# Output weights' third unit, the opening's sum of squares and the order of weighing in the attention core rearranged

## The chip, the cores and the metric

The kernel runs on one core of one Trainium2 chip. The metric is the device time of one execution in microseconds (us), the median of several runs. A matrix engine (PE), a vector engine (DVE), a scalar engine (ACT), a general engine (POOL) and a queue that starts transfers (SP) work side by side, each through its own instructions in order, and wait for each other by semaphores.

## What is computed

An encoder trunk of two layers on 272 tokens (256 and 16 learned meta tokens) of width 1024. Layer 0 is FFN, attention (16 query heads, 4 key/value heads of 64, rotary positions), FFN; layer 1 is FFN, a recurrent block, FFN. Cut to what matters here:

```python
h = concatenate([meta, x])                       # 272 x 1024
for layer in range(2):
    h = h + 0.5 * rms_norm(swiglu(rms_norm(h, g[0]), ffn_w_in, ffn_w_out), g[1])
    hn = rms_norm(h, g[2])                       # layer 0: attention
    q, k, v = split(hn @ w_qkv)
    q, k = rope(rms_norm(q, q_gain)) / 8, rope(rms_norm(k, k_gain))
    o = softmax(q @ k.T) @ v                     # 16 heads
    h = h + rms_norm(o @ w_o, g[3])
    h = h + 0.5 * rms_norm(swiglu(rms_norm(h, g[4]), ffn_w_in, ffn_w_out), g[5])
```

All arrays are float32. `rms_norm` needs the mean of the squares of h over the 1024 channels of each token.

## The kernel before

Activations lie with channels on the 128 partitions: `h[:, c, :]`, c = 0 to 7, holds 272 tokens. A product in full precision is made of three matmuls of split operands (`product`, L473 to L475): a high part (xh, wh) and a low part (xl, wl). Weights come in units of up to 1 MB through a ring of four slots: SP loads `raw`, ACT copies it to `wh` (`high`, L981), DVE subtracts to get `wl` (`low`, L1394), and PE multiplies. A slot is loaded again when the `low` of its last unit is done. U_QKV+0 to +5 are the six units of the q, k and v weights, U_WO+0 to +3 the four of the output weights.

**Opening.** ACT splits h and the first four units and squares the eight tiles of h (`h_square`, L993) into a buffer of two; POOL adds the squares one after the other into `hacc` (`sum_squares`, L1887 and L1890). PE takes the mean over the partitions (`mean_of_h`, L527) behind the gate half of the third tile of the first FFN and goes on with the up half, inside which it spreads the reciprocal root over the partitions (`spread_r`, L520). The scaled tiles (L1463, L1464) that free PE's banks need that spread.

**Queries and keys.** Tiles t = 0 to 9 (two of keys, eight of queries) are multiplied in order; inside the product of a later tile PE takes the head means (`head_means`, L727) and the rotation (`rotate`, L737) of an earlier one. DVE follows per tile with `head_root_in`, `times_sin`, `head_factor`, ACT with `squared` and `root`, POOL with `times_cos` and `roped`. Copies and subtractions of later weight units are set between these by hand: `low(U_QKV + 4, 0)` after t = 3, `high(U_WO, ...)` before `root(4)`.

**Attention core.** 18 steps. Steps 0 and 9 treat the 16 last query rows of eight heads; the other 16 are pairs of steps, two token halves of one tile of two heads. Step s on PE: `scores(s + 2)` (L764, or L756 for steps 0 and 9), `turn(s)` (six transposes of the softmax rows, three in steps 0 and 9, L775), `weigh(s - 1)` (values times probabilities, 12 records, L787). Step s on DVE: `normalise(s)` (L1657, L1661), for every second step `out_split` (L1665, L1667), then `maximum(s + 2)` (L1644) and `shifted(s + 2)` (L1652). Step s on ACT: `exponents(s + 1)` (L1215), then `place(s)` (L1234; L1227 and L1228 for steps 0 and 9). `scores(s)` waits for `exponents(s - 2)`, the second half of `turn(s)` for `place(s - 1)`, `weigh(s)` for `place(s)`, and `place(9)` for all of the first eight weighings. In the last two steps PE begins the output projection between turns (`begin_wo`). The third output unit is copied by ACT in step 0 and subtracted by DVE in step 10, where DVE also clears `acc` (L1421).

Of the kernel before, what the change touches and what calls it, by code (L numbers as in the profile page):

```python
# [9 lines left out]
ALU = mybir.AluOpType  # L10
# [7 lines left out]
KC = D // P  # L18
# [54 lines left out]
STEPS_S = 9  # L73
# [81 lines left out]
def build(nc, x, meta, gains, ffn_in, ffn_out, w_qkv, q_gain, k_gain, w_o, rec_in, conv_w, conv_b,  # L155
          gate_w, gate_b, lam, rec_out, consts, out):
    ctx = ExitStack()
    with ctx:
# [309 lines left out]
        def _(pe):  # L468
# [230 lines left out]
            def attention():  # L699
# [150 lines left out]
                for s in range(STEPS):  # L850
                    if s + 2 < STEPS:
                        scores(s + 2)
                    if s == 0:
                        pe.wait_ge(q_step, 3 * QKT - 2)
                        pe.wait_ge(q_sin, QKT)
                        pe.wait_ge(v_ready, 2)
                    if s >= STEPS - 2:
                        begin_wo(3 * (s - STEPS + 2), 3 * (s - STEPS + 2) + 3)
                    turn(s)
                    if s == 0:  # L860
                        pe.wait_ge(v_ready, 4)
                    if s >= 1 and (s - 1) % STEPS_S:
                        weigh(s - 1)
                begin_wo(6, 7)
                weigh(STEPS - 1)

            def begin_wo(k0, k1):
# [107 lines left out]
        def _(act):  # L975
# [12 lines left out]

            def h_square(n, c):
                t0 = PROJ_T0[n - 1] if n else 0  # L990
                if 8 * n + c >= 2:
                    act.wait_ge(hacc_step, 8 * n + c - 1)
                act.activation(sqh[:, c % 2, t0:L], h[:, c, t0:L], ACT.Square).then_inc(hsq_ready, 1)  # L993

            def make_x(n):

# [160 lines left out]
            def attention():  # L1157
                def squared(t):

                    act.wait_ge(qk_done, t + 1)  # L1160
                    if t >= 2:
                        act.wait_ge(q_sum, t - 1 if t % 2 or t == 2 else t)
                    for a, cols in row_parts(t) if t >= KT_N else ((t % 2 * L, slice(0, L)),):
                        last = act.activation(qs_row[:, a:a + cols.stop - cols.start], qk_bank(t)[:, cols], ACT.Square)
                    last.then_inc(q_squared, 1)
                    if t >= 2:
                        act.wait_ge(q_rot, t - 1)
                        act.wait_ge(q_cos, t - 1)
                    g = 1 if t < KT_N else 0
                    act.activation(qp[:, t % 2, :], qk_bank(t)[:, 0:L], ACT.Copy, scale=qg[:, g:g + 1]).then_inc(q_gained, 1)  # L1170

                def root(t):
                    act.wait_ge(q_step, 3 * t + 1)
                    if t < KT_N:
                        v = hs[:, t].rearrange("p c g -> p (c g)")
                    else:
                        a, n = factor_columns(t)
                        v = hq[:, a:a + n]
                    act.activation(v, v, ACT.Sqrt, bias=EPS).then_inc(q_root, 1)

                squared(0)
                squared(1)
                root_of_h(1)
                high(U_QKV + 4, 0, KC, (qk_done, 4))
                act.wait_ge(norm_q_sum, 1)
                act.activation(rc_q[:, :], SUM_PRE[:, SC + 3:SC + 8], ACT.Sqrt, bias=EPS).then_inc(norm_q_root, 1)
                root(0)
                squared(2)
                root(1)
                squared(3)  # L1190
                high(U_QKV + 5, 0, KC, (qk_done, 4))
                root(2)
                squared(4)
                root(3)
                squared(5)
                high(U_WO, 0, KC, (qk_done, 6))
                root(4)
                squared(6)
                root(5)
                root(6)  # L1200
                squared(7)
                high(U_WO + 1, 0, KC, (qk_done, 8))
                root(7)
                squared(8)
                root(8)
                squared(9)
                root(9)
                load_table(ACT.Exp)

                def exponents(s):  # L1210
                    act.wait_ge(shift_ready, s + 1)
                    if s >= 2:
                        act.wait_ge(t_done, first_tile(s - 1))
                    for e, a in enumerate(range(first_tile(s), first_tile(s + 1))):
                        act.activation(prow[:, 2 * (s % 2) + e, :], SCORE[s % 2][:, e, 0:L], ACT.Exp,  # L1215
                                       scale=hq[:, factor_column(a):factor_column(a) + 1], bias=shift[:, a:a + 1],
                                       accum_out=rsum[:, a:a + 1]).then_inc(p_exp, 1)

                def place(s):

                    p, q = divmod(s, STEPS_S)
                    act.wait_ge(t_done, first_tile(s + 1))
                    if q == 0:
                        if p:
                            act.wait_ge(pv_done, 4 * p)
                        src = flipped[0:KT, TURN[s][0][1], 0:3 * P].rearrange("p (c j g q) -> p c j g q", c=3, j=2, g=GROUP)
                        act.activation(pt[:, 0, :, :, 2 * P:L], src[:, :, 0], ACT.Copy)  # L1227
                        act.activation(pt[:, 1, :, :, 2 * P:L], src[:, :, 1], ACT.Copy).then_inc(pt_ready, 1)  # L1228
                    else:
                        j, i, half = pair_of(s)  # L1230
                        b0, b1 = sorted(b for e, b, placed in TURN[s])
                        src = flipped[0:KT, b0:b1 + 1, 0:3 * P].rearrange("p g (c q) -> p g c q", c=3)
                        dst = pt[:, j % 2, :, i:GROUP:2, P * half:P * half + P].rearrange("p c g q -> p g c q")
                        act.activation(dst, src, ACT.Copy).then_inc(pt_ready, 1)  # L1234

                exponents(0)
                for s in range(STEPS):
                    if s + 1 < STEPS:
                        exponents(s + 1)
                    if s == 0:  # L1240
                        high(U_WO + 2, 0, KC, (qk_done, 10))
                    place(s)
                high(U_WO + 3, 0)
                load_table(ACT.Sqrt)
# [113 lines left out]
                x_high(0, c)  # L1358
            high_half(1, 0)
            high_half(1, 1)  # L1360
            h_square(0, 0)
            h_square(0, 1)
            high(2, 0)
            high(3, 0)
            for c in range(2, KC):
                h_square(0, c)
            ffn(0, True)

# [20 lines left out]
        def _(dve):  # L1389
# [13 lines left out]
            def rc_of_h(n):  # L1403
                dve.wait_ge(pre_root, n + 1)
                dve.reciprocal(rc_pre[:, :], rc_pre[:, :]).then_inc(rc_ready, 1)
# [166 lines left out]
            def attention():  # L1572
# [30 lines left out]
                def final(t):  # L1603
# [5 lines left out]
                dve.wait_ge(hacc_step, 8 * 1 + 8)  # L1609
                dve.tensor_copy(hrest[:, :].rearrange("p (i m) -> p i m", i=2),  # L1610
                                hacc[:, L - META:L].rearrange("p (o m) -> p o m", o=1).broadcast_to([P, 2, META])).then_inc(rest_doubled, 1)
                rc_of_h(1)
                dve.wait_ge(rc_ready, 2)
                dve.tensor_tensor(rsq[:, :], rc_pre[:, :], rc_pre[:, :], ALU.mult).then_inc(rsq_ready, 1)
# [7 lines left out]
                for t in range(QKT - 1):  # L1622
                    head_root_in(t)
                    times_sin(t)
                    head_factor(t)
                    if t == 1:
                        final(0)
                    if t == 2:
                        final(1)
                    if t == 3:  # L1630
                        low(U_QKV + 4, 0)
                    if t == 5:
                        low(U_QKV + 5, 0)
                    if t in (6, 7):
                        low(U_WO + t - 6, 0)
# [37 lines left out]
                head_factor(QKT - 1)  # L1673
                maximum(1)
                shifted(1)
                value(0)
                value(1)
                for s in range(STEPS):
                    normalise(s)
                    if s == 0:  # L1680
                        value(2)
                        dve.wait_ge(v_ready, 3)
                        dve.memset(vt[0:OVERLAP, 2, :], 0.0).then_inc(v_ready, 1)
                    if s == 10:
                        low(U_WO + 2, 0)
                        clear_sum()
                    if s >= 2 and (s - 2) % STEPS_S:
                        j, i, half = pair_of(s - 2)
                        if half:
# [142 lines left out]
            def low_half(u, i):  # L1832
# [3 lines left out]
                last = dve.tensor_tensor(wl[:, slot(u), cols], raw[:, slot(u), cols], wh[:, slot(u), cols].bitcast(F32), ALU.subtract)  # L1836
                last.then_inc(w_ready if i else w_half, 1)

            def copy_h(c):
                dve.wait_ge(x_trans, c + 1)  # L1840
                dve.tensor_copy(h[:, c, :], bank[4 + c % 4][:, 0:L]).then_inc(h_ready, 1)
# [15 lines left out]
            dve.tensor_scalar(vec_h[:, :], vec_a[:, :], 0.5, None, ALU.mult).then_inc(vec_ready, 1)  # L1857
            low(2, 0)
            low(3, 0)

            ffn(0, True)
            attention()
# [13 lines left out]
        def _(pool):  # L1876
            def sum_squares(n):

                t0 = PROJ_T0[n - 1] if n else 0
                if n:  # L1880
                    pool.wait_ge(pre_sum, n)
                if n == 2:
                    pool.wait_ge(norm_q_sum, 1)
                for c in range(KC):
# [59 lines left out]
                y_sum(2)  # L1944
                y_gated(2)

            sum_squares(0)
            sum_squares(1)
            rotary()
            sum_squares(2)  # L1950
# [30 lines left out]
```

## Time and profile before

| | |
|---|---|
| median of 3 runs | 1075.98 us (1074.69 to 1076.16) |
| the profiled execution | 1076.33 us, its span 1074.5 us |
| PE busy | 1055.3 us, 98% of the span |
| DVE, ACT, POOL busy | 683.3, 545.4, 91.3 us |
| moved by transfers | 170.15 MB, mean 158 GB/s |
| mean granted clock of PE | 0.996 of full |

The span is from the first to the last instruction of the profiled execution. Times in the rows are microseconds from its start. A busy PE is not one at its peak: the modelled end of a matmul lies behind the start of the next, so durations of PE blocks are best taken from start to start.

### The profile page before, as it was taken

How to read it: one execution, taken by the hardware profiler on the slowest of the kernel's cores; microseconds unless marked ns; L12 is line 12 of the kernel's file. 1: busy time of each engine (PE TensorE's matmuls, PEld its weight loads, DVE VectorE, ACT ScalarE, POOL GpSimd, SP SyncE). 2: the span in 40 equal slices, each digit the busy share in tenths (PEclk: the TensorE clock that was granted, in tenths of full speed). 3: DMA queues.
4: the chain of work that ended last, by engine and by line, in shares of the span. 5: the costliest groups of instructions: out<-in, count | busy, mean ns of one | idle time of the engine just before them, and what ended most of it. 6: DMA issues, size and time to landing. Idle time of an engine off the chain costs nothing.

```text
span 1074.5 us, 20606 instructions
## 1 busy us (share of the span) xinstructions
PE 1055.3 (98%) x8416; PEld 1026.4 (96%) x8416; DVE 683.3 (64%) x991; ACT 545.4 (51%) x790; POOL 91.3 (8%) x92
## 2 busy tenths in 40 slices
PE   9999999999989999999999999999999999999997
PEld 8899999999879999999999999999999999999986
DVE  6566656467664866664457666644698668667652
ACT  5544444454765544444346444444569845454541
POOL 2100000028000200000011000000223310000000
PEclk9999999999989999999999999999999999999999
DMA  9465446625013255435563555366328525655541
GB/s 301 154 225 165 137 138 209 218 89 175 27 41 123 95 188 185 156 122 188 193 204 118 173 193 164 108 203 217 118 80 269 162 80 182 200 167 197 189 143 39
DMA packets 160910, 170.15 MB, mean 158 GB/s; under 512 B 3264, under 2 KB 154104, under 8 KB 160840
## 3 DMA queue, kind: packets, MB, share of 16 engines
q1 hardware_dynamic: 160456, 168.70, 48.0%
q8 instruction: 51, 0.84, 0.3%
q0 software_dynamic: 96, 0.28, 0.1%
q10 hardware_dynamic: 288, 0.18, 0.1%
q14 instruction: 19, 0.16, 0.0%
HBM read 167.82 MB, written 1.05 MB: 157 GB/s over the span
## 4 chain that ended last, share of the span: by engine, by line
PE 89%; DVE 4%; ACT 2%; DMA 2%; SPq 1%; POOL 1%; issue 1%; DVEq 0%; POOLq 0%; ACTq 0%
PE bank L473 23%; PE bank L475 23%; PE bank L474 23%; PE bank L882 5%; PE bank L681 2%; PE bank L680 2%; PE bank L682 2%; PE weighed L787 1%; PE bank L492 1%; PE bank L489 1%; PE flipped L775 1%; PE bank L490 1%; DMA raw<-in_ffn_w_in 1%; DVE h L1436 1%; DMA raw<-in_rec_w_in 1%; POOL hacc L1890 1%
## 5 line engine op out<-in xcount | busy, mean ns | idle before, releaser
L1394 DVE TENSOR_TENSOR wl<-raw,wh 128x2048 fp32r<-128x2048 f32 (+2 forms) x164 | 340.5, 2097 | 152.7 <-ACT wh L981 152.2
L473 PE MATMUL bank<-xh,wl 128*128 128x272 f32 (+1 forms) x1488 | 431.1, 290 | 3.4 <-DVE tmp L1464 1.1
L475 PE MATMUL bank<-xh,wh 128*128 128x272 f32 (+1 forms) x1488 | 428.0, 288 | 0.0
L474 PE MATMUL bank<-xl,wh 128*128 128x272 f32 (+1 forms) x1488 | 426.3, 286 | 0.0
L981 ACT ACTIVATE wh<-raw 128x2048 fp32r<-128x2048 f32 (+2 forms) x164 | 282.2, 1745 | 104.6 <-PE bank L475 82.9
L473 PEld LDWEIGHTS bank<-xh,wl 128*128 128x128 f32 x1488 | 280.9, 189 | 5.2 <-issue 2.7
L474 PEld LDWEIGHTS bank<-xl,wh 128*128 128x128 f32 x1488 | 281.0, 189 | 0.0
L475 PEld LDWEIGHTS bank<-xh,wh 128*128 128x128 f32 x1488 | 280.7, 189 | 0.0
L473 PE MATMUL bank<-ah,wl 128*128 128x272 f32 x528 | 152.5, 289 | 0.0
L474 PE MATMUL bank<-al,wh 128*128 128x272 f32 x528 | 152.2, 288 | 0.0
L475 PE MATMUL bank<-ah,wh 128*128 128x272 f32 x528 | 151.8, 287 | 0.0
L1047 ACT ACTIVATE tmp<-tmp 128x272 f32<-128x272 f32 (+1 forms) x88 | 37.7, 428 | 215.3 <-DVE tmp L1463 215.0
L474 PEld LDWEIGHTS bank<-al,wh 128*128 128x128 f32 x528 | 99.5, 188 | 0.0
L473 PEld LDWEIGHTS bank<-ah,wl 128*128 128x128 f32 x528 | 99.5, 188 | 0.0
L475 PEld LDWEIGHTS bank<-ah,wh 128*128 128x128 f32 x528 | 99.4, 188 | 0.0
L1482 DVE TENSOR_TENSOR al<-tmp,ah 128x272 f32 (+3 forms) x88 | 38.2, 438 | 51.0 <-ACT ah L1052 50.4
L1463 DVE TENSOR_TENSOR tmp<-bank,r 128x272 f32<-128x272 f32 (+1 forms) x88 | 38.1, 433 | 50.4 <-PE bank L475 50.3
L1887 POOL COPY hacc<-sqh 128x272 f32<-128x272 f32 (+1 forms) x6 | 2.9, 488 | 700.4 <-ACT sqh L993 700.4
L1052 ACT ACTIVATE ah<-tmp 128x272 f32 (+3 forms) x88 | 37.4, 428 | 47.4 <-DVE tmp L1472 47.4
L489 PE MATMUL bank<-xh,wl 128*128 128x272 f32 (+1 forms) x176 | 46.1, 290 | 2.3 <-ACT xh L987 1.7
L1472 DVE TENSOR_TENSOR tmp<-tmp 128x272 f32<-128x272 f32 (+1 forms) x88 | 38.2, 437 | 13.6 <-ACT tmp L1047 9.2
L490 PE MATMUL bank<-xh,wh 128*128 128x272 f32 (+1 forms) x176 | 45.6, 287 | 0.0
(199 smaller groups left out, 1207.7 us busy)
## 6 DMA issues: line engine op xcount, KB each, us to landing
raw<-in_ffn_w_in SPq DMA_DIRECT2D x88, 1024.0 KB, 5.3
raw<-in_ffn_w_out SPq DMA_DIRECT2D x24, 768.0 KB, 4.4
raw<-in_ffn_w_out SPq DMA_DIRECT2D x24, 640.0 KB, 3.8
raw<-in_ffn_w_out SPq DMA_DIRECT2D x10, 1024.0 KB, 5.2
raw<-in_rec_w_in SPq DMA_DIRECT2D x8, 1024.0 KB, 5.5
raw<-in_attn_w_qkv SPq DMA_DIRECT2D x6, 1024.0 KB, 5.0
raw<-in_attn_w_o SPq DMA_DIRECT2D x4, 1024.0 KB, 5.0
raw<-in_rec_gate_w SPq DMA_DIRECT2D x16, 256.0 KB, 5.0
```

Source lines behind the costliest of these rows:

```text
L473: pe.matmul(dst, b, mh, start=first, stop=False)
L474: pe.matmul(dst, a, ml, start=False, stop=False)
L475: return pe.matmul(dst, a, mh, start=False, stop=last)
L489: pe.matmul(dst, b, xh[:, k, t0:L], start=k == 0, stop=False)
L490: pe.matmul(dst, a, xh[:, k, t0:L], start=False, stop=False)
L882: done = pe.matmul(dst[:, cols], w, x[:, cols], start=first and half == 0, stop=last, skip_group_check=True)
L981: act.activation(wh[:, slot(u), 0:kn * 256], raw[:, slot(u), 0:kn * 256], ACT.Copy).then_inc(wh_ready, units)
L1047: act.activation(sl[:, b, t0:L], gp[:, b, t0:L], ACT.Silu).then_inc(silu_done, 1)
L1394: dve.tensor_tensor(wl[:, slot(u), 0:kn * 256], w, wh[:, slot(u), 0:kn * 256].bitcast(F32), ALU.subtract).then_inc(w_ready, units)
L1463: dve.tensor_tensor(gp[:, b, t0:L], bank[banks[0]][:, t0:L], r[:, t0:L], ALU.mult).then_inc(gate_scaled, 1)
L1472: dve.tensor_tensor(aa[:, b, t0:L], sl[:, b, t0:L], up[:, b, t0:L], ALU.mult).then_inc(a_full, 1)
L1482: dve.tensor_tensor(d, aa[:, b, t0:L], s, ALU.subtract).then_inc(a_ready, 1)
```

## The change

In the opening, the squares of h go to eight places of `tmp` without waiting for one another, all of them behind the copies of units 2 and 3; DVE adds them in three instructions (`first_sum`) behind its subtractions of units 2 and 3, and POOL no longer takes part. In the q and k stage, `root(4)` stands ahead of `high(U_WO)` on ACT and `low(U_QKV + 4)` moves behind tile 4 on DVE. `clear_sum` moves to the beginning of the attention stage. The third output unit's copy moves ahead of `root(9)` on ACT, its subtraction ahead of `value(0)` on DVE. In the core, PE weighs the two halves of a tile one right behind the other: nothing in the first step of a pair's weighing, two in the second.

```diff
-                    if s >= 1 and (s - 1) % STEPS_S:
+                    q = (s - 1) % STEPS_S
+                    if s >= 1 and q and q % 2 == 0:
+                        weigh(s - 2)
                         weigh(s - 1)
                 begin_wo(6, 7)
+                weigh(STEPS - 2)
                 weigh(STEPS - 1)
...
             def h_square(n, c):
                 t0 = PROJ_T0[n - 1] if n else 0
-                if 8 * n + c >= 2:
-                    act.wait_ge(hacc_step, 8 * n + c - 1)
-                act.activation(sqh[:, c % 2, t0:L], h[:, c, t0:L], ACT.Square).then_inc(hsq_ready, 1)
+                if n:
+                    act.wait_ge(hacc_step, 8 * n + max(c - 1, 0))
+                dst = sqh[:, c % 2, t0:L] if n else tmp[:, c, :]
+                act.activation(dst, h[:, c, t0:L], ACT.Square).then_inc(hsq_ready, 1)
...
                 squared(5)
+                root(4)
                 high(U_WO, 0, KC, (qk_done, 6))
-                root(4)
...
                 squared(9)
+                high(U_WO + 2, 0, KC, (qk_done, 10))
                 root(9)
...
-                    if s == 0:
-                        high(U_WO + 2, 0, KC, (qk_done, 10))
                     place(s)
...
-            h_square(0, 0)
-            h_square(0, 1)
             high(2, 0)
             high(3, 0)
-            for c in range(2, KC):
+            for c in range(KC):
                 h_square(0, c)
...
+                clear_sum()
                 rc_of_h(1)
...
-                    if t == 3:
+                    if t == 4:
                         low(U_QKV + 4, 0)
...
                 shifted(1)
+                low(U_WO + 2, 0)
                 value(0)
...
-                    if s == 10:
-                        low(U_WO + 2, 0)
-                        clear_sum()
...
+            def first_sum():
+
+                dve.wait_ge(hsq_ready, KC)
+                dve.tensor_tensor(tmp[:, 0:4, :], tmp[:, 0:4, :], tmp[:, 4:8, :], ALU.add).then_inc(hacc_step, 1)
+                dve.wait_ge(hacc_step, 1)
+                dve.tensor_tensor(tmp[:, 0:2, :], tmp[:, 0:2, :], tmp[:, 2:4, :], ALU.add).then_inc(hacc_step, 1)
+                dve.wait_ge(hacc_step, 2)
+                dve.tensor_tensor(hacc[:, :], tmp[:, 0, :], tmp[:, 1, :], ALU.add).then_inc(hacc_step, KC - 2)
...
             low(2, 0)
             low(3, 0)
+            first_sum()
...
-            sum_squares(0)
             sum_squares(1)
```

## Rows read from the trace of the kernel before

**Rows 1.** The page, part 4: share of the last chain by engine.
```profile
PE 89%; DVE 4%; ACT 2%; DMA 2%; SPq 1%; POOL 1%; issue 1%; DVEq 0%; POOLq 0%; ACTq 0%
```

**Rows 2.** PE's waits, whole span: total us, times, longest us.
```profile
PE flipped L775 <- DVE prow L1661: 2.9, 2, 2.5
...
PE bank L473 <- DVE tmp L1464: 1.1, 1, 1.1
...
PE score_odd L764 <- ACT prow L1215: 0.4, 1, 0.4
```

**Rows 3.** Timeline of the opening: start, us, instruction, count, idle before and releaser.
```profile
19.97 1.92 ACT L981 ACTIVATE wh<-raw 128x2048 fp32r<-128x2048 f32 x1 [0.47 <-DMA raw<-in_ffn_w_in]
21.79 0.73 ACT L993 ACTIVATE sqh<-h 128x272 f32<-128x272 f32 x2
...
21.87 4.48 DVE L1394 TENSOR_TENSOR wl<-raw,wh 128x2048 fp32r<-128x2048 f32 x2
...
22.28 9.26 POOL L1890 TENSOR_TENSOR hacc<-hacc,sqh 128x272 f32<-128x272 f32 x6 [3.43 <-ACT sqh L993]
...
29.87 0.29 PE L475 MATMUL bank<-xh,wh 128*128 128x272 f32 x1
31.60 0.67 PE L527 MATMUL bank<-cst,hacc 128*96 128x1 f32 x6 [1.44 <-POOL hacc L1890]
```

**Rows 4.** Timeline of the q and k stage, DVE and PE.
```profile
251.13 2.28 DVE L1394 TENSOR_TENSOR wl<-raw,wh 128x2048 fp32r<-128x2048 f32 x1
...
252.89 0.29 PE L475 MATMUL bank<-xh,wh 128*128 128x272 f32 x1
253.63 0.58 PE L727 MATMUL bank<-cst,tmp 128*128 128x2 f32 x4 [0.45 <-DVE hq L1581]
```

**Rows 5.** Timeline of DVE and PE around step 10, and where the projection begins.
```profile
300.22 2.28 DVE L1394 TENSOR_TENSOR wl<-raw,wh 128x2048 fp32r<-128x2048 f32 x1
...
305.01 1.49 PE L775 MATMUL flipped<-cst,prow 128*96 128x128 f32 x6 [2.52 <-DVE prow L1661]
...
318.47 0.40 PE L473 MATMUL bank<-xh,wl 128*128 128x272 f32 x1
```

**Rows 6.** Stretches: length; PE, PEld, DVE, ACT, POOL busy; clock; transfers' share; GB/s.
```profile
282.00:298.00 16.00, 15.86 (x184) 12.04 (x182) 13.63 (x43) 13.40 (x35) 0.00 (x0) 1.00 0.01 2
...
304.00:308.00 4.00, 2.99 (x20) 2.28 (x20) 2.57 (x10) 2.69 (x8) 0.00 (x0) 0.51 0.73 251
```

**Rows 7.** Timeline of DVE and ACT where the moved work comes to stand.
```profile
237.16 0.17 DVE L1405 RECIPROCAL rc_pre<-rc_pre 96x3 f32<-96x3 f32 x1 [2.14 <-ACT rc_pre L1003]
...
273.68 0.16 DVE L1652 TENSOR_TENSOR shift<-nmax,hq 128x2 f32<-128x2 f32 x1
275.91 0.87 DVE L1639 TENSOR_SCALAR vt<-bank,rc_pre 96x256 f32<-96x256 f32 x2 [2.08 <-PE bank L803]
...
270.73 0.21 ACT L1179 ACTIVATE hq<-hq 128x5 f32<-128x5 f32 x1 [1.62 <-DVE hq L1581]
```

**Rows 8.** Timeline of PE in the core: undisturbed steps, then step 9.
```profile
286.47 0.73 PE L764 MATMUL score_even<-kd,qt 64*128 64x136 f32 x8
287.13 0.86 PE L775 MATMUL flipped<-cst,prow 128*96 128x128 f32 x6
287.92 0.88 PE L787 MATMUL weighed<-pt,vt 96*64 96x128 f32 x12
288.73 0.73 PE L764 MATMUL score_odd<-kd,qt 64*128 64x136 f32 x8
...
298.52 0.53 PE L775 MATMUL flipped<-cst,prow 128*96 128x128 f32 x3
298.99 0.96 PE L787 MATMUL weighed<-pt,vt 96*64 96x144 f32 x12
```

**Rows 9.** Groups by shape, 282 to 298 us: count, busy us, mean ns, idle before.
```profile
L1234 ACT ACTIVATE pt<-flipped 96x768 f32<-96x768 f32 x8 | 6.4, 806 | 2.8 <-PE flipped L775 2.8
L1215 ACT ACTIVATE prow<-score_even,shift,hq 128x272 f32<-128x272 f32 x7 | 3.9, 569 | 0.0
```

More of the change, by code:

```diff
@@ L1877, in sum_squares @@
             def sum_squares(n):
-                t0 = PROJ_T0[n - 1] if n else 0
-                if n:
-                    pool.wait_ge(pre_sum, n)
+                t0 = PROJ_T0[n - 1]
+                pool.wait_ge(pre_sum, n)
                 if n == 2:
```

## The prediction

> **What bounds the kernel now.** I read the chain of waits first: 89% of the chain that ended last is PE [rows 1]. So an edit pays only where it shortens PE's own work or one of its stalls, and the next view is PE's list of waits [rows 2]: the longest is for the normalised softmax rows, 2.9 us in two waits, 2.5 in one. Then I read the timeline at each stall that the change touches.
>
> In the opening, PE's mean of the squares starts at 31.60 after 1.44 idle, released by POOL, whose six last additions take 9.26 us from 22.28 [rows 3]. In the q and k stage PE is held 0.45 for DVE's root input, which stood behind the subtraction of a unit (251.13, 2.28 us) [rows 4]. In the core the 2.52 before the turn of step 11 ends at 305.01, and DVE's step 10 began with a subtraction of 2.28 us at 300.22 [rows 5]. After that idle stretch the granted clock in 304 to 308 is 0.51, near the 1.2 GHz level, so the stall is paid again in slow matmuls [rows 6].
>
> **Opening.** Without the wait the mean would start one matmul spacing behind 29.87; spacing there is 0.13 us (0.29 is the modelled duration, with overlap), so at 30.00, against 31.60: 1.60 us. Will the sum be ready? ACT's copy of unit 3 waits for its transfer and runs 19.97 to 21.79 (start of the next); eight squares at the spacing of 0.31 that two of them show (0.73 in all, 0.43 for one) take 2.6, to 24.4. DVE is busy with units 2 and 3 until 26.35, so DVE decides. Its three additions have 1088, 544 and 272 elements a partition. The trace has 2048 in 2.24 each (4.48 for two) and small ones of 272 at about 0.44; on a line between them these are 1.26, 0.72 and 0.44, with dependency gaps 2.5 us in all: `hacc` at 28.9, 1.1 before PE wants it. The copies of units 2 and 3 and their subtractions don't get later, because two squares leave ACT ahead of them. Everything behind the mean hangs on PE's own place in its program (the spread stands at the sixth product of the up half), so the 1.1 wait for the scaled tile [rows 2] stays and only moves. Bounds: 1.44 (the idle time only) to 1.60; I take 1.60.
>
> **Queries and keys.** The mean at 253.63 would follow 252.89 by 0.13: 0.61 us to gain. With unit QKV+4 moved behind tile 4, `head_root_in(4)` runs at once at 251.2, `times_sin(4)` to 251.8, `root(4)` no longer behind a 1.9 us copy; all before PE arrives at 253.02. The subtraction then runs from about 252.1 to 254.4. Its weights are wanted by tile 8, behind the mean, rotation and the 27 matmuls left of tiles 6 and 7 (3.4), so not before 257.5. The next root input waits for the subtraction, to 254.4, while PE asks for it 12 matmuls (1.5) into tile 7, near 256. What POOL does meanwhile may be held up by the two-input subtraction as it was before, with over a microsecond to spare. Bounds 0.45 to 0.61; I take 0.60.
>
> **Clearing and the third output unit.** The clear (0.28 us) falls into DVE's 2.14 idle before 237.16 [rows 7]: nothing. On ACT the copy (1.9) stands ahead of the last root, which began at 270.73 [rows 7]: the copy takes the place of the 1.62 idle before it, and the root comes about 0.2 later than it could. Its user is the normalisation of the first softmax row, which stands behind two values that wait for PE: hidden. On DVE the subtraction starts after the shift of step 1 (273.68 [rows 7], now 0.6 earlier) and needs 2.28 to 275.4, and DVE's next instruction there waited 2.08 for PE anyway: nothing. If that cover failed, up to the length of the subtraction, 2.2, less PE's slack before its first turn, would come back.
>
> **The stall in the core.** Blocks from start to start: scores 0.66, turn 0.79, weighing of a first half 0.81 [rows 8], of a second half 0.89 (16 more columns in 12 records). The weighing at 298.99 ends 0.89 later, at 299.87. From there to the projection at 318.47 [rows 5] PE has six scores and turns, 6 x 1.45 = 8.70, and five weighings, 3 x 0.81 + 2 x 0.89 = 4.21: 12.91 us. One wait of about 0.4 for the exponents of step 11 [rows 2] isn't DVE's doing and stays. 299.87 + 12.91 + 0.42 = 313.20, so stall and slow clock together cost 318.47 - 313.20 = 5.27 us. All of it goes if nothing takes its place; bounds 4.9 to 5.7 (the second if the 0.4 goes too).
>
> **Weighing in one run.** A turn of three transposes takes 0.47 (298.52 to 298.99), one of six 0.79 [rows 8]: 0.107 a transpose, and 0.15 once per block. The weighings likewise: 0.08 for 12 x 16 columns makes 5 ns for 12 columns, 12 x 128 columns are 0.64, so 0.17 per block is not columns; scores, 8 x 136, 0.45 of 0.66, leave 0.21. The six-transpose turn has a satisfied wait in its middle and pays nothing for it, so I put the 0.15 to 0.21 down to the change of shape between blocks, not to the waits. Two weighings, one right behind the other, drop one such change per tile: 8 x 0.17 = 1.36 us. Ends: 0 (if it belongs to the wait, which is kept) and 8 x 0.21 = 1.7.
> The Trainium skill, page "TensorEngine Tiling (Array Packing)", section Key Properties, says that changing the tiling mode, not the tile alone, drains the engine. By that rule the sum is as above; if the 0.17 belonged to the waits it would be 1.36 us higher. The rows agree with the rule as far as they go.
>
> Against it: PE has no weighing in the first step of a pair, and runs ahead of ACT and DVE. An ACT step is two exponents and their accumulator reads, 2 x 0.55 from start to start, and a placing of 0.81 (0.70 to the next) [rows 9], 1.8 us; two steps 3.6, against PE's 4.5 per tile: enough in the steady state. There turn to turn in the short step is 1.45, and the second half of the turn, 1.85 behind the last one's start, needs a placing that ends 0.90 + 0.81 = 1.71 behind it: 0.14 to spare. But at each of the two starts (steps 1 to 3 and 10 to 12) no earlier weighing covers the exponents, and PE now has one step more of 1.45 against ACT's 1.8 before its first weighing: it must wait 0.35 more, with the semaphore's way some 0.39, at the scores of step 3 and of step 12. Loss 2 x 0.39 = 0.78 us, bounds 0.2 (slack that I don't see) to 1.6 (each start pays twice).
>
> **Sum.** 1.60 + 0.60 + 5.27 + 1.36 - 0.78 = 8.05 us. The profiled execution's 1076.33 becomes 1068.3; it lies 0.35 above the median of 1075.98, so the median becomes 1068.0 rounded. Later stages are PE's and should only move: the transfer of the FFN's third unit starts earlier, since the slot is freed near 275.4 instead of 302.5.
>
> **Rivals.**
> A. *The short steps starve.* If the 0.17 belongs to the wait (+1.36) and each of the six other tiles also stands about 0.39 (+2.3), the time is 1071.7. For it: ACT is busy 13.4 of 16 us [rows 6], and the margin above is 0.14. Against: PE's steady period is still longer than ACT's.
> B. *The opening's sum is late.* If the additions started behind a later unit 3 or ran slower than the line says, PE's wait returns from 1.1 us of delay on, and whole from 2.7, which gives 1069.6. DVE's chain has 1.1 of slack, but rests on a transfer.
> C. *The moved unit hits the start of the core.* If its copy comes so late that the subtraction delays the values and the first turn, of its 2.2 us some 1.7 return (an estimate: PE's last 24 value matmuls hide the rest): 1069.7. For it: ACT's queue there is full (copy, root, table, exponents). Against: DVE's 2.08 of waiting [rows 7].
> D. *Slower.* PE's many small idle pieces in the new order let its clock fall to 1.2 GHz in the core. The trace shows the fall after 2.52 idle [rows 5, 6], with 5.27 - 2.52 = 2.75 us paid besides the idle time. The core's PE work is some 16 x 2.3 = 37 us; from 8.05 us of it at half clock the gain is gone, from 10.2 us the kernel is slower by 0.2%, a third of the core (12 us) gives 1080. Against: waits of 0.4 and 1.1 [rows 2] left the clock at full, and none of mine is above 0.4.
> That the change doesn't do what it says: only if the step 11 turn waits for something behind the subtraction; ACT's exponents 11 are the 0.4 already counted.
>
> **How the numbers follow.** Forecast 0.66, A 0.15, B 0.08, C 0.07, D 0.04. A measurement of this kernel tells about 0.2% (2.2 us) from no change. Worst ends of the terms: 1.44 + 0.45 + 4.9 + 0 - 1.6 = 5.2, time 1070.8; best: 1.60 + 0.61 + 5.7 + 1.7 - 0.2 = 9.4, time 1066.6. B and C lie inside; A and D, 0.19, are left out. Faster: all but D, 0.95 with a little taken off for mixtures; same 0.02, slower 0.03.
>
> **What would show it.** PE's wait for POOL in the opening gone and its mean at 30.0; no wait for DVE near 253; no subtraction in step 10 and the granted clock at full through the core; projection from about 310 (8.05 us less what comes after); weighing runs of 24 records in 1.53 us start to start; waits of 0.4 for exponents at steps 3 and 12 only. Wrong: a 24-record run of 1.70, waits for placings in every second turn, a clock below 1.00 between 276 and 322, or a wait for DVE's values at the first turn.

## The result, and the profile after

The changed kernel takes 1068.05 us (median of 4 runs, 1067.55 to 1068.81) against 1075.95 for the kernel before in the same set: a ratio of 0.993, 95% interval 0.9912 to 0.9947. The forecast was 1068.0. The profiled execution took 1068.51 us, 7.82 less than the one before. So the total was met; the terms behind it were not all.

PE's waits in the changed kernel (total us, times, longest us), which answer to [rows 2]:

```profile
...
PE flipped L775 <- ACT pt L1239: 1.2, 4, 0.4
PE bank L473 <- DVE tmp L1465: 1.1, 1, 1.1
PE bank L473 <- DVE xl L1669: 1.1, 1, 1.1
...
PE score_odd L764 <- ACT prow L1220: 0.7, 2, 0.4
PE flipped L775 <- DVE prow L1663: 0.4, 1, 0.4
...
PE score_even L764 <- ACT prow L1220: 0.3, 1, 0.3
```

The three waits that the change aimed at are gone: POOL's sum, DVE's root input, the 2.5 us in step 11. New are four waits for a placing, 1.2 in all, and two for exponents (the kernel before had one of 0.4). The rows left out stand in both kernels. The wait of 0.6 for the second unit's low part (L489) is no longer listed either.

**Opening.** Timeline of the changed kernel, against [rows 3]:

```profile
15.40 3.38 DVE L1401 SCALAR_TENSOR_TENSOR xl<-h,vec_a,xh 128x272 fp32r<-128x272 f32 x8
...
21.09 4.48 DVE L1395 TENSOR_TENSOR wl<-raw,wh 128x2048 fp32r<-128x2048 f32 x2
25.49 1.28 DVE L1842 TENSOR_TENSOR tmp<-tmp 128x1088 f32<-128x1088 f32 x1
26.81 0.73 DVE L1844 TENSOR_TENSOR tmp<-tmp 128x544 f32<-128x544 f32 x1
27.64 0.44 DVE L1846 TENSOR_TENSOR hacc<-tmp 128x272 f32<-128x272 f32 x1
...
21.02 2.66 ACT L997 ACTIVATE tmp<-h 128x272 f32<-128x272 f32 x8
...
29.21 0.59 PE L527 MATMUL bank<-cst,hacc 128*96 128x1 f32 x6
```

The sum costs DVE what was worked out (1.28, 0.73, 0.44) and is there 1.1 before PE. But the mean starts at 29.21, not at 30.00. The larger part of the difference stands in two rows of the kernel before that the prediction had not looked at:

```profile
15.49 4.07 DVE L1400 SCALAR_TENSOR_TENSOR xl<-h,vec_a,xh 128x272 fp32r<-128x272 f32 x8
...
20.75 0.39 PE L489 MATMUL bank<-xh,wl 128*128 128x272 f32 x1 [0.62 <-DVE wl L1836]
```

The eight low parts of x took DVE 0.69 longer there, and PE stood 0.62 for the unit subtracted behind them.

This is one pair of traces. Five experiments below keep the opening of the kernel before (e5, e6, e8, e10, e12). From the first low part of x to the mean, e5 and e12 take 16.08 and 16.11, like the 16.11 of the kernel before; e6, e8 and e10 take 15.45, 15.43 and 15.45, and in them the mean waits for POOL only 0.74 to 0.78. In the three slower ones POOL's first addition of the last six lasts 4.5 to 4.7, behind both subtractions of DVE. In the other three the copy of unit 3 did not wait for its transfer, and that addition was over in 0.77, when the subtractions began. The new opening takes 13.81 to 13.83 in every trace that has it. So it is worth 1.6 to 2.3, depending on the run.

**Queries and keys**, against [rows 4]:

```profile
248.88 0.20 ACT L1183 ACTIVATE hq<-hq 128x4 f32<-128x4 f32 x1 [0.34 <-DVE hq L1582]
...
250.50 2.28 DVE L1395 TENSOR_TENSOR wl<-raw,wh 128x2048 fp32r<-128x2048 f32 x1
...
250.56 0.50 PE L727 MATMUL bank<-cst,tmp 128*128 128x2 f32 x4
```

The head mean at 253.63 now starts at 250.56, 3.07 earlier. Of this 2.46 had been gained ahead of it (the mean of the tile before moved from 250.61 to 248.15); the rest is 0.61, as forecast.

**Core.** PE in the steady part, against [rows 8]:

```profile
283.61 0.73 PE L764 MATMUL score_even<-kd,qt 64*128 64x136 f32 x8
284.27 0.86 PE L775 MATMUL flipped<-cst,prow 128*96 128x128 f32 x6
285.06 0.73 PE L764 MATMUL score_odd<-kd,qt 64*128 64x136 f32 x8
286.09 0.83 PE L775 MATMUL flipped<-cst,prow 128*96 128x128 f32 x6 [0.29 <-ACT pt L1239]
286.85 1.61 PE L787 MATMUL weighed<-pt,vt 96*64 96x128 f32 x24
288.39 0.73 PE L764 MATMUL score_even<-kd,qt 64*128 64x136 f32 x8
```

The run of two weighings takes 1.54 start to start against 0.81 + 0.89, 0.16 saved. But the scores of the short step last 1.03 to the next turn instead of 0.66, and the tile takes 4.78 instead of 4.60. The stretch that held the stall, against [rows 6]:

```profile
304.00:308.00 4.00, 3.71 (x44) 2.84 (x41) 3.34 (x10) 3.02 (x10) 0.00 (x0) 1.00 0.00 0
```

The clock is at its full level (2.4 GHz).

One measure serves for the core from here on: the stretch from PE's scores of step 2 to its first product behind the last output split. Its ends are 278.62 and 329.42 before, 275.47 and 321.61 after, so 50.80 and 46.14 us. The 7.82 of the two profiled executions are then 2.39 in the opening, 0.07 on the way to the q and k stage, 0.61 in it, 0.08 on the way to the core and 4.66 in the core (7.81).

### The profile page after: what moved, and what is told of

Same layout as the page of the kernel before. It is cut to its first block, busy times and chain, and to the rows that moved or that the text cites. A ratio compares the mean times of both kernels' runs of the same rounds, so it can differ in the third digit from the quotient of the medians.

```text
span 1066.7 us, 20595 instructions
## 1 busy us (share of the span) xinstructions
PE 1050.5 (98%) x8416; PEld 1024.2 (96%) x8416; DVE 685.0 (64%) x994; ACT 544.2 (51%) x790; POOL 81.2 (8%) x84
## 3 DMA queue, kind: packets, MB, share of 16 engines
HBM read 167.82 MB, written 1.05 MB: 158 GB/s over the span
## 4 chain that ended last, share of the span: by engine, by line
PE 90%; DVE 4%; ACT 3%; DMA 1%; issue 0%; SPq 0%; DVEq 0%; ACTq 0%
PE bank L473 23%; PE bank L475 23%; PE bank L474 23%; PE bank L885 4%; PE bank L681 2%; PE bank L680 2%; PE bank L682 2%; PE bank L492 1%; PE bank L489 1%; DMA raw<-in_rec_w_in 1%; PE bank L490 1%; PE weighed L787 1%; DVE xl L1401 1%; PE flipped L775 1%; DVE h L1437 1%; PE bank L520 1%
## 5 line engine op out<-in xcount | busy, mean ns | idle before, releaser
L489 PE MATMUL bank<-xh,wl 128*128 128x272 f32 (+1 forms) x176 | 45.9, 289 | 1.9 <-ACT xh L990 1.7
```

What stands on the lines that cost most here:

```text
L489: pe.matmul(dst, b, xh[:, k, t0:L], start=k == 0, stop=False)
```

## The experiments

Where a trace is quoted, the stretch is the one just defined. The changed kernel ran once more beside the last set (**e9_changed_again**):

> The changed kernel itself, beside the others of this set. 1068.0, its stretch from the scores of step 2 to the product behind the last output split 46.1 us as before.

1068.27 us (1067.52 to 1068.96, 5 runs); stretch 321.28 - 275.16 = 46.12.

**e5_unit_only**: the kernel before with the moved unit and clearing alone.

```diff
                 squared(9)
+                high(U_WO + 2, 0, KC, (qk_done, 10))
                 root(9)
...
-                    if s == 0:
-                        high(U_WO + 2, 0, KC, (qk_done, 10))
...
+                clear_sum()
                 rc_of_h(1)
...
                 shifted(1)
+                low(U_WO + 2, 0)
...
-                    if s == 10:
-                        low(U_WO + 2, 0)
-                        clear_sum()
```

> The kernel before with only the third output unit (its copy on ACT, its subtraction on DVE) and the clearing moved. Theory of the stall: 5.27 us less, 1070.7, no wait before the turn of step 11, clock at full through the core, the first output product 5.3 earlier than 318.5. Rival: another wait in steps 10 to 12 takes its place and only part of it goes, over 1072.

1070.28 us (1070.11 to 1071.82), ratio 0.9954 (0.9938 to 0.9971). The stretch is 324.81 - 279.14 = 45.67, so 5.13 less than before. The list of waits has none left at the turn of step 11. The rival falls.

Three of its runs took 1070.11 to 1070.29, with a mean clock of 1.000; the profiled one took 1071.82, with 0.998. Its trace shows the difference, and it lies in the opening:

```profile
30.61 0.67 PE L527 MATMUL bank<-cst,hacc 128*96 128x1 f32 x6 [1.41 <-POOL hacc L1888]
...
32.00:34.00 2.00, 2.00 (x12) 2.00 (x11) 0.00 (x0) 1.98 (x2) 0.00 (x0) 0.52 0.07 20
34.00:36.00 2.00, 2.00 (x14) 2.00 (x13) 0.00 (x0) 0.81 (x2) 0.00 (x0) 0.62 0.00 0
```

Behind the wait of 1.41 for POOL's sum the clock fell to the 1.2 GHz level for some 3 us. From the mean to the scores of step 2 this run takes 279.14 - 30.61 = 248.53, the kernel before 278.62 - 31.60 = 247.02: the fall cost 1.5. In the kernel before the same wait of 1.44 left the clock at full:

```profile
32.00:34.00 2.00, 2.00 (x19) 2.00 (x19) 0.17 (x1) 1.70 (x2) 0.00 (x0) 1.00 0.29 89
```

**e1_alternate**: the changed kernel with the old order of weighing.

```diff
-                    q = (s - 1) % STEPS_S
-                    if s >= 1 and q and q % 2 == 0:
-                        weigh(s - 2)
+                    if s >= 1 and (s - 1) % STEPS_S:
                         weigh(s - 1)
                 begin_wo(6, 7)
-                weigh(STEPS - 2)
                 weigh(STEPS - 1)
```

> The changed kernel with PE's old order of weighing, one half a step; all else of the change stays. Theory P (as predicted): the run of two saves 1.36 us of shape changes and costs 0.78 in two waits, so without it the time goes up 0.6, to 1068.6. Theory W (from the changed kernel's trace): the run of two saves 0.16 a tile, 1.3 in all, but PE then stands 0.29 to 0.36 in four short turns (steps 5, 7, 9, 14) and about 0.7 in two starts, 1.9 in all; without it the time falls 0.6, to 1067.4. In the trace, from the scores of step 2 to the first product behind the last output split: P 46.7, W 45.5, the changed kernel 46.1. W also wants the four waits for placings gone.

The stretch is 320.79 - 275.12 = 45.67, and the waits for placings are gone; 1067.69 us (1067.59 to 1068.55). Theory W holds in direction. So the run of two cost 0.47 in the core, where the prediction had counted on a gain of 0.58. In time alone this can't be told (1067.69 against 1068.05 and 1068.27); the traces tell it.

**e2_mixed**: as e1, but the last two tiles in runs of two.

```diff
-                    q = (s - 1) % STEPS_S
-                    if s >= 1 and q and q % 2 == 0:
+                    if 1 <= s < STEPS - 3 and (s - 1) % STEPS_S:
+                        weigh(s - 1)
+                    if s == STEPS - 2:
                         weigh(s - 2)
                         weigh(s - 1)
```

> As e1_alternate, but the last two tiles (steps 14 and 15, 16 and 17) are weighed in one run, where PE has output products between the turns to cover ACT and DVE. Theory W: the two runs save 2 x 0.16 and cost nothing, so 0.3 below e1_alternate, 1067.1, with the stretch at 45.2. Theory P: each run of two pays everywhere, so still above the changed kernel, about 1068.3.

The stretch is 320.40 - 275.44 = 44.96; 1067.48 us (1067.39 to 1068.20), which the time alone can't tell from e1. The direction is W's, but the stretch is 0.71 below e1's, more than twice the 0.3 expected. The rows of step 15 show why. e1_alternate:

```profile
308.25 0.86 PE L775 MATMUL flipped<-cst,prow 128*96 128x128 f32 x6
309.04 0.88 PE L787 MATMUL weighed<-pt,vt 96*64 96x128 f32 x12
309.85 0.39 PE L473 MATMUL bank<-xh,wl 128*128 128x272 f32 x1
```

e2_mixed:

```profile
308.57 0.86 PE L775 MATMUL flipped<-cst,prow 128*96 128x128 f32 x6
309.19 0.37 PE L473 MATMUL bank<-xh,wl 128*128 128x272 f32 x1
```

A turn ahead of a weighing lasts 0.79 to the next start, one ahead of a product 0.62, which is no more than six times 0.107. From transposes to products (both on the whole array, 128 rows) nothing is paid. So with no weighing between them two changes of shape fall away instead of one: 0.17 + 0.17 for each of the two tiles, 0.7 in all. Both kinds of block stand behind a wait for a semaphore that holds nothing up here, so the 0.15 to 0.21 per block belongs to the change of shape and not to the wait. The Trainium skill, page "TensorEngine Tiling (Array Packing)", section Key Properties, has it that changing the mode, not the tile, drains the engine; the runs agree.

**e7_no_low_part**: which engine ends the wait in the short step?

```diff
+                    if pair < 2 * NKV - 1:
+                        dve.tensor_copy(xh[:, pair, :], weighed[:, 0:L]).then_inc(o_ready, 1)
+                        return
                     dve.tensor_copy(xh[:, pair, :], weighed[:, 0:L]).then_inc(oh_ready, 1)
...
```

> Leaves out the low part of the attention output (the subtraction at the output split) for all but the last tile, 0.44 us of DVE in every second step; the rest is the changed kernel. It tells which engine ends PE's wait in the short turns of steps 5, 7, 9 and 14. If it is DVE's normalisation, which stands behind output split and maximum, the waits of 0.29 to 0.36 shrink or go. If it is ACT's placing of the step before, which begins only when the turn before ends, they stay whole.

1069.82 us in its one run, which can't be set against the others; the stretch is 321.43 - 275.94 = 45.49, 0.65 less than in the changed kernel. Its timeline around step 5 (PE, DVE, ACT):

```profile
285.53 0.73 PE L764 MATMUL score_odd<-kd,qt 64*128 64x136 f32 x8
286.40 0.83 PE L775 MATMUL flipped<-cst,prow 128*96 128x128 f32 x6
...
284.86 0.72 DVE L1646 TENSOR_REDUCE nmax<-score_even 128x2 f32<-128x544 f32 x1 [0.22 <-PE score_even L764]
...
285.89 0.63 DVE L1663 TENSOR_SCALAR prow<-prow,rinv 128x272 f32<-128x272 f32 x2
...
285.64 0.81 ACT L1239 ACTIVATE pt<-flipped 96x768 f32<-96x768 f32 x1 [0.99 <-PE flipped L775]
```

For comparison DVE and ACT in the changed kernel, whose turn starts at 286.09:

```profile
283.73 0.44 DVE L1667 CAST xh<-weighed 128x272 fp32r<-128x272 f32 x1 [0.48 <-PE weighed L787]
...
285.58 0.63 DVE L1663 TENSOR_SCALAR prow<-prow,rinv 128x272 f32<-128x272 f32 x2
...
285.17 0.81 ACT L1239 ACTIVATE pt<-flipped 96x768 f32<-96x768 f32 x1 [0.98 <-PE flipped L775]
```

In e7 the turn starts at 286.40 while the placing still runs (to 286.45): its first half doesn't need it. It needs the first normalised row, which ends near 286.25. In the changed kernel both ended together (placing 285.98, normalised row 285.94), and the profile names the later; with less DVE work the scores' 1.03 became 0.87, and the maximum now waited for PE's scores instead of for DVE. So DVE's chain behind the run of two decides: output split 0.83, then maximum, shift, reciprocal and normalisation. In the changed kernel the turn starts 286.09 - 283.61 = 2.48 behind the end of the run of two, where PE's own way would be 0.66 + 0.79 + 0.66 = 2.11: 0.37 too late. All four waits shrank by 0.16 or so in e7, which makes its 0.65. The 0.21 that is left of each is DVE's too: the maximum stands ahead of the normalisation that the turn needs, and waits for PE's scores. Whether the placing of ACT would hold the turn's second half once DVE is out of the way was not tested.

**e8_weigh_only**: the kernel before with the run of two alone (the same edit as in the change).

> The kernel before with the weighing in runs of two as its only edit. Theory P: 0.6 faster, 1075.4. Theory W: 0.6 slower, 1076.5, with the waits for placings at the same steps; the big stall before the turn of step 11 stays about 2.5 long, since DVE's unit is still in step 10, and the clock falls as before.

1073.84 us (1072.23 to 1077.70, 10 runs), ratio 0.9995 (0.9982 to 1.0008): neither P nor W can be told from it, since its runs differ by more than both. The four waits for placings are there, and the stall is 1.98 long. And a part of my expectation failed: in the profiled run the clock did not fall.

```profile
304.00:306.00 2.00, 1.50 (x14) 1.14 (x14) 1.93 (x7) 1.78 (x5) 0.00 (x0) 1.00 1.04 365
```

In the kernel before, the same two microseconds:

```profile
304.00:306.00 2.00, 0.99 (x5) 0.97 (x6) 1.90 (x8) 1.23 (x4) 0.00 (x0) 0.53 0.97 333
306.00:308.00 2.00, 2.00 (x17) 1.31 (x15) 0.68 (x3) 1.47 (x4) 0.00 (x0) 0.50 0.48 169
```

The runs of the kernel before say the same. Over the four sets of experiments there are 55: three with a mean clock of 1.000 took 1072.64 to 1073.38, the 23 with 0.996 took 1075.19 to 1076.85, the four with 0.994 took 1076.99 to 1077.54. So the time has a part that comes with the clock and changes from run to run. To part it from the waiting:

**e10_busy_stall** and **e12_busy_short**: the kernel before with 18 or 10 matmuls of no use in the stall.

```diff
+                    if s == 11:
+                        pe.wait_ge(pt_ready, 9)
+                        keep_warm(10, flipped[:, 0, :])
                     turn(s)
```

> The kernel before with 18 matmuls of no use (128 columns each, 2.3 us) on PE inside the 2.5 us stall ahead of the turn of step 11; nothing waits for them. If part of the 5.27 us of the stall's price is the slow clock behind the idle time, the granted clock stays at full and the time falls by what the clock cost: 2.75 us in the profiled execution, about 1073.0, and the runs lie closer together than the 4.5 us by which the kernel before spreads. If the stall's price is all waiting, the time stays at 1075.5.

1076.13 us (1075.21 to 1077.70), ratio 1.0007. The clock stayed at full through the core in its trace (the mean over the whole execution is 0.998 or 0.999 in all 11 runs), but I had the filler's length wrong: such a matmul makes two records of 0.115, so 18 take 4.12 us and outlast the stall by 1.5.

> As e10_busy_stall with 10 matmuls of no use instead of 18. In e10 each took 0.229 us (two records of 128 columns), 4.1 us in all, 1.5 past the stall's end, which hid what the clock gave back; 10 take 2.3 and end inside the stall. If the clock is part of the price, it stays at full, the stretch from the scores of step 2 to the product behind the last output split falls from 50.8 to about 48.1, and the runs are near 1073.3, no wider apart than 2 us. If it is not, they stay at 1075.5 with the kernel before.

```profile
302.83 2.50 PE L481 MATMUL flipped<-cst 128*128 128x128 f32 x20
305.42 0.83 PE L775 MATMUL flipped<-cst,prow 128*96 128x128 f32 x6
```

```profile
304.00:306.00 2.00, 1.91 (x18) 1.75 (x17) 1.93 (x6) 1.16 (x4) 0.00 (x0) 1.00 0.89 269
306.00:308.00 2.00, 2.00 (x26) 1.52 (x24) 1.28 (x6) 1.78 (x5) 0.00 (x0) 1.00 0.73 253
```

Stretch 327.13 - 279.03 = 48.10, as expected: 2.70 less than before, with the stall as long. The median is 1074.07 against 1075.70, ratio 0.9988 (0.9978 to 0.9997). The runs lie from 1072.19 to 1075.65, wider than the 2 us I had set. The trace, taken of the slowest run (1075.65), shows two of the things that vary. Its opening is like that of e5: a wait of 1.42 for POOL's sum, then a clock of 0.52 and 0.62 in 32 to 36, and 1.5 more from the mean to the scores of step 2 (248.55 against 247.02). And later, in the recurrent block, PE waits 2.4 for ACT (`gr`, L1262), where the kernel before waits 0.8; why is open. With the start of the stretch 0.41 later, the 2.70 and the 1.6 this gives the 0.68 between the two profiled executions.

**e6_qk_only**: the kernel before with the two moves of the q and k stage alone (the same lines as in the change).

> The kernel before with only root(4) ahead of the copy of unit WO and the subtraction of unit QKV+4 behind tile 4. The head mean at 253.63 comes 0.6 earlier, 253.0, without a wait, and the scores of step 2 at 278.0 against 278.62; time 1075.3, which one run can't tell from 1076.

Its wait for the root input is gone. Its one run took 1073.85, which can't be told from the kernel before; the mean of the squares came at 30.86 in it, not 31.60, so its absolute times can't be set against those expected. The clock fell in it too, but for less long: its stretch is 326.81 - 277.17 = 49.64.

**e3_pool_sum** and **e4_pool_late**: the changed kernel with POOL's sum, first with the two early squares, then with all squares behind the unit copies.

```diff
...
+            h_square(0, 0)
+            h_square(0, 1)
             high(2, 0)
             high(3, 0)
-            for c in range(KC):
+            for c in range(2, KC):
                 h_square(0, c)
...
             low(3, 0)
-            first_sum()
...
+            sum_squares(0)
             sum_squares(1)
```

> The changed kernel with the old opening (two squares ahead of the unit copies, POOL adds). By the predicted term the time goes up by 1.6, to 1069.65; by the two traces (mean at 31.60 against 29.21) by 2.4, to 1070.45, since PE also gets its old 0.62 wait for the second unit's low part back.

1070.47 us (1070.14 to 1071.51), ratio 0.996 (0.9946 to 0.9974): 2.4 above the changed kernel's 1068.05, not 1.6. But that compares two sets of runs, and two of the five (1071.35 and 1071.51) have a mean clock of 0.997 against 0.999. Its own trace says less: from the first low part to the mean 30.55 - 14.78 = 15.77, 1.96 more than the 13.81 of the changed kernel. The wait of 0.62 is back as expected, the one for POOL is 1.08.

> As e3_pool_sum, but all eight squares stand behind the copies of units 2 and 3, so POOL does nothing while DVE makes the eight low parts of x. If POOL's first copy and addition held DVE up there (4.07 us against 3.38), the low parts take 3.4 and PE's 0.62 wait for the second unit is gone although POOL still sums; if the order of ACT's work made the difference alone, the low parts... take 3.4 only if DVE waited for ACT, and their single instructions are 0.5 in both. The mean comes later than 31.6, since POOL begins at 21.4 against 17.4.

(That sentence on the order of ACT's work is not well put; what was to be seen is the length of the eight low parts.) e3, then e4:

```profile
14.78 4.06 DVE L1402 SCALAR_TENSOR_TENSOR xl<-h,vec_a,xh 128x272 fp32r<-128x272 f32 x8
...
20.03 0.39 PE L489 MATMUL bank<-xh,wl 128*128 128x272 f32 x1 [0.62 <-DVE wl L1837]
```

```profile
15.31 3.38 DVE L1400 SCALAR_TENSOR_TENSOR xl<-h,vec_a,xh 128x272 fp32r<-128x272 f32 x8
...
19.88 0.39 PE L489 MATMUL bank<-xh,wl 128*128 128x272 f32 x1 [0.16 <-DVE wl L1835]
32.16 0.67 PE L527 MATMUL bank<-cst,hacc 128*96 128x1 f32 x6 [2.88 <-POOL hacc L1898]
```

In e4 POOL still sums, but not while DVE makes the low parts: they take 3.38, and the wait falls to 0.16. So it was POOL's instruction at that moment that held DVE. The times fit: in e3 the long low part runs from 17.42 to 18.43, beside POOL's addition from 17.35 to 18.13, after ACT's two squares have ended at 16.98; ACT's copy of unit 2 runs beside the low parts in both. The longest single low part is 1015 ns in the kernel before and 497 in e4. It works the other way too: of POOL's six last additions before, which met DVE's subtractions [rows 3], one lasted 4.7 us against 0.78 for the others. The Trainium skill, page "SBUF — State Buffer", section Who interferes with whom, says that a DVE instruction with two SBUF inputs contends with a GpSimd instruction that reads SBUF; both directions agree with it.

**e11_mixed_spread**: what the runs point to, e2_mixed with the spread of the root moved up, since the root is now ready early.

```diff
-                            if f == f0 + 2 and (part, k) == ((0, 3) if n else (1, 6)):
+                            if f == f0 + 2 and (part, k) == ((0, 3) if n else (1, 3)):
```

> e2_mixed with the opening's spread of the reciprocal root after the fourth product of the up half instead of the seventh. With the squares summed early the root is there at 30.2, the fourth product ends near 31.2: PE's wait of 1.1 for the scaled tile should go, and the time fall from 1067.5 to 1066.4. If DVE or the root isn't ready, the wait only moves to the spread and the time stays.

```profile
29.06 0.59 PE L527 MATMUL bank<-cst,hacc 128*96 128x1 f32 x6
31.09 0.80 PE L520 MATMUL bank<-cst,rc_pre 96*128 96x96 f32 x6
```

1065.96 us (1065.71 to 1066.35), ratio 0.9911 (0.9896 to 0.9926), 2.3 below the changed kernel in the same set, with no run in common. The 1.1 wait for the scaled tile is gone, and the stretch is 44.96, 1.16 less than in e9: together the 2.3. It beats both kernels.

## Why the prediction was right, and where only its sum was

**Opening: 1.60 forecast, 2.3 measured in the two profiled executions, 1.6 against three other traces of the old opening.** From the first low part of x to the mean PE took 31.60 - 15.49 = 16.11 before and 29.21 - 15.40 = 13.81 after; the other 0.09 is an earlier start. The step that it rested on, one matmul spacing instead of the wait, held, and the sum came with the 1.1 to spare that was worked out. Missing was that POOL's early copy and addition had lengthened DVE's work (0.69) while PE waited for it (e3, e4). I had priced what POOL's part ended, not what it did to others while it ran. This held-up work is in every trace of the old opening (0.62 of waiting in each). That the forecast of 1.60 fits three of them is luck: there the wait for POOL, which it took as fixed at 1.44, is 0.74 to 0.78. Nor did it count the slow clock that followed this wait in e5 and e12 for 1.5 more, and which the change removes with the wait. (The spread stands behind the seventh product, k = 6, not the sixth; nothing hangs on it.) Rival B fell: the wait did not return.

**Queries and keys: 0.60, measured 0.61.** Both the wait and its removal came as worked out.

**Third unit: 5.27, measured 5.13** (e5). The block sum from start to start was good to 0.14. The clock's share, worked out as 2.75, measured 2.70 (e12); the rest, 2.43, is waiting. But it was taken as a fixed cost, and it isn't: e6 paid 1.16 less of it (49.64 against 50.80), e8 none of the clock's share, and the runs of the kernel before with a mean clock of 1.000 are some 2.8 faster than those with 0.996. That the profiled execution from which it was read had the fall in the core and none in the opening, and lay near the median, was luck. Rival C fell: DVE's values started right behind the subtraction, and PE did not wait for them.

**Runs of two: +0.58 forecast, -0.47 measured** (e1). The saving was sized too low: 0.16 for each of six tiles and 0.71 for the last two (e2) are 1.67, not 1.36. The loss was 0.78 in the forecast and 1.67 + 0.47 = 2.14 in fact. From start to start, the two starts lose 0.43 and 0.34, near the 0.39 forecast for each; the rest is four short turns (steps 5, 7, 9, 14) with 0.34, 0.40, 0.33 and 0.33; the sum is 2.17. The step that failed is "0.14 to spare" in the steady state: it looked at ACT's placing alone and left out DVE's chain from output split to normalisation, which now begins only after the run of two and brings the next turn 0.37 later than PE would be there (e7). The sign that the prediction had named for being wrong, waits for placings at the turns, came with it. Rival A had the place and nearly the price per tile (0.39), but put it down to ACT, let all six other tiles pay, and had the saving fall away too; the saving stayed whole, so A's 1071.7 was never near.

**Clock.** Rival D didn't come: through the core, with idle pieces of up to 0.4, the clock stayed at full in every trace of the changed kernel and its variants. (In e4 it fell in the opening, to 0.52 and 0.63 in 34 to 38, behind the wait of 2.88.)

The errors of the sum, for the two profiled executions: 0.70 too little in the opening and 0.09 of an earlier start, 0.15 between the stages, 0.01 in the queries and keys, 0.14 too much for the stall, 1.05 too much for the runs of two. They nearly cancel (7.81 against 8.05), and the time fell on the forecast. That is luck; the two large errors have nothing to do with each other. The range of 1066.6 to 1070.8 would have held the time with either error alone.

## What to carry to other kernels

When two dependent blocks are drawn together to save a changeover, follow every engine's chain from the end of the longer block to the next instruction that waits, not the nearest one only: the saving of 0.16 was paid for with 0.34 wherever the next step was short, and kept where other work stood between. An instruction moved off POOL can give back more than the wait that it ended; look for instructions of one shape with two durations. An idle stretch of the matrix engine like the 1.4 and 2.5 us here can cost as much again in slow matmuls, in some runs and not in others: take such a term with a range, read it from more than one trace, and compare stretches of a trace beside medians.

## What the runs showed of the hardware that was not expected

- How long PE idled does not settle whether its clock fell. Behind 2.52 us of idle it was at the half level (1.2 GHz) for about 6 us in the kernel before (0.53, 0.50, 0.50, 0.77 in the four stretches of 2 us from 304) and for some 3 us in e6 behind the same stall. Behind 1.98 in the trace of e8 it stayed at full. Behind 1.41 and 1.42 in the openings of e5 and e12 it fell (0.52, 0.62 in 32 to 36), behind 1.44 in the kernel before it did not. With PE filled by useless matmuls in the stall, it was at full through the core in the traces of e10 and e12.
- Transposes of 96 columns followed by 128-column products cost no changeover (0.62 for six); transposes followed by 64-column weighings cost 0.17.
- A DVE instruction of 0.49 us took up to 1.02 beside a POOL addition, and a POOL addition of 0.78 took 4.7 beside DVE's subtractions of two 2048-column units: it was held through both.
